# Norms of a second transformer stack: the root and the reciprocal taken per token as columns, the factor spread by a product with the identity

## What is computed

```python
def rms_norm(x, g):
    xf = x.astype(jnp.float32)
    y = xf * lax.rsqrt(jnp.mean(xf * xf, axis=-1, keepdims=True) + NORM_EPS)
    return (y * g.astype(jnp.float32)).astype(x.dtype)
def modulate(h, shift, scale):
    return h * (1 + scale) + shift
# in layer l of the second stack (ctx is only carried on in layer 0):
h  = modulate(rms_norm(x, g_mix[l]), sh1, sc1)      # 512 tokens, 1024 features
hc = modulate(rms_norm(ctx, g_mix[l]), csh1, csc1)  # 256 tokens, 1024 features
# rms_norm of c_q (384 features) and of c_kv (128 features), for x and for ctx
# modulate(rms_norm(x, g_ffn[l]), ...) before the feed-forward part
return rms_norm(x, g_final)
```

## Time and profile before

| | |
|---|---|
| median of 3 runs | 3974.38 us (3973.16 to 3976.8) |
| the profiled execution's own time | 3969.17 us |
| its span from the first to the last instruction | 3967.4 us |
| mean granted TensorE clock | 0.956 |
| PE busy | 3636.3 us, 92% |
| PEld busy | 2914.2 us, 73% |
| DVE busy | 2221.1 us, 56% |
| ACT busy | 1364.0 us, 34% |
| chain that ended last | PE 76%, DVE 12%, ACT 5% |

### The profile page before, as it was taken

One profiled execution on the slowest core, in us unless ns is written; L12 is line 12 of the kernel. 1 busy time (PEld: TensorE's weight loads), 2 busy tenths in 40 slices (PEclk: granted clock), 3 DMA queues, 4 the chain that ended last, 5 costly groups with the idle time before them and its releaser, 6 DMA issues.

```text
span 3967.4 us, 53234 instructions
## 1 busy us (share of the span) xinstructions
PE 3636.3 (92%) x19180; PEld 2914.2 (73%) x19180; DVE 2221.1 (56%) x3260; ACT 1364.0 (34%) x2104; POOL 190.7 (5%) x157
## 2 busy tenths in 40 slices
PE   8988999999998899999967998899999879879997
PEld 6755787888786578788846775688888657657876
DVE  7864456445686544744566553563535665545445
ACT  5544433222445443322212334142323233324322
POOL 2300000000230000000000000000000000000000
PEclk9988999999998999999978998999999989989998
DMA  3233332222223323222211001111111110112221
GB/s 131 85 139 120 115 113 100 96 95 95 85 86 139 139 100 113 98 95 98 94 58 53 22 21 49 43 53 64 64 64 64 54 64 22 49 64 85 93 87 74
DMA packets 44792, 325.32 MB, mean 82 GB/s; under 512 B 5088, under 2 KB 5344, under 8 KB 6112
## 3 DMA queue, kind: packets, MB, share of 16 engines
q1 hardware_dynamic: 43920, 315.88, 21.9%
q10 hardware_dynamic: 720, 7.40, 0.5%
HBM read 321.16 MB, written 2.10 MB: 81 GB/s over the span
## 4 chain that ended last, share of the span: by engine, by line
PE 76%; DVE 12%; ACT 5%; issue 3%; DVEq 3%; DMA 1%; ACTq 0%; SPq 0%
PE psum L663 10%; PE psum L665 10%; PE psum L664 10%; PE psum L1000 10%; PE psum L1002 10%; PE psum L1001 10%; PE psum L1113 3%; PE psum L1088 3%; ACT whi L1223 2%; PE psum L1099 2%; DVE wlo L1616 2%; DVE MA L1743 2%; PE psum L704 2%; PE psum L767 1%; PE psum L719 1%
## 5 line engine op out<-in xcount | busy, mean ns | idle before, releaser
L1223 ACT ACTIVATE whi<-wst 128x2048 fp32r<-128x2048 f32 x248 | 473.7, 1910 | 787.2 <-PE psum L1002 384.2
L1616 DVE TENSOR_TENSOR wlo<-wst,whi 128x2048 fp32r<-128x2048 f32 x216 | 495.0, 2291 | 197.5 <-ACT whi L1223 196.1
L663 PE MATMUL psum<-xh,whi 128*128 128x512 f32 x1328 | 525.3, 396 | 35.2 <-issue 15.1
L665 PE MATMUL psum<-xh,wlo 128*128 128x512 f32 x1328 | 519.9, 391 | 0.0
L664 PE MATMUL psum<-xl,whi 128*128 128x512 f32 x1328 | 519.7, 391 | 0.0
L1000 PE MATMUL psum<-xh,whi 128*128 128x512 f32 x944 | 380.4, 403 | 52.7 <-DVE xl L2046 40.1
L1001 PE MATMUL psum<-xl,whi 128*128 128x512 f32 x944 | 373.8, 396 | 0.0
L1002 PE MATMUL psum<-xh,wlo 128*128 128x512 f32 x944 | 373.3, 395 | 0.0
L663 PEld LDWEIGHTS psum<-xh,whi 128*128 128x128 f32 x1328 | 251.1, 189 | 99.2 <-issue 47.9
L665 PEld LDWEIGHTS psum<-xh,wlo 128*128 128x128 f32 x1328 | 251.0, 189 | 53.2
L664 PEld LDWEIGHTS psum<-xl,whi 128*128 128x128 f32 x1328 | 251.2, 189 | 52.6 <-issue 1.0
(11 more groups left out here) (300 smaller groups left out, 6570.7 us busy)
## 6 DMA issues: line engine op xcount, KB each, us to landing
wst<-weights SPq DMA_DIRECT2D x296, 1024.0 KB, 4.8
dft<-c_dft ACTq DMA_DIRECT2D x2, 2688.0 KB, 9.0
hT<-x_t SPq DMA_DIRECT2D x4, 512.0 KB, 7.5
out<-hT SPq DMA_DIRECT2D x1, 2048.0 KB, 6.3
masks<-c_masks SPq DMA_DIRECT2D x1, 1024.0 KB, 12.4
cT<-ctx_t ACTq DMA_DIRECT2D x1, 1024.0 KB, 6.4
ropes<-c_ropes ACTq DMA_DIRECT2D x1, 512.0 KB, 7.1
sm<-small ACTq DMA_DIRECT2D x1, 314.0 KB, 2.8
```

The lines of the kernel that those rows point to most:

```text
L663: pe.matmul(ps[bank][:, :], w_hi, rh[:, k + k0, :], start=n == 0, stop=False)
L665: last = pe.matmul(ps[bank][:, :], w_lo, rh[:, k + k0, :], start=False, stop=n == len(kts) - 1)
L1223: act.activation(m.whi[:, slot, :], m.wst[:, slot, :], ACT.Copy).then_inc(s.hi_ready, 1)
L1616: TT(m.wlo[:, slot, :], m.wst[:, slot, :], m.whi[:, slot, :].bitcast(F32), ALU.subtract).then_inc(s.lo_ready, 1)
```

## The change

Sums come out as columns: for each block b of 128 tokens the squares are the stationary operand and one column of ones is the moving one, which gives a 128x1 column with the tokens on the partitions. Mean, root and reciprocal work on 128x4 (or 128x2). Then PE, still inside `sums2`, waits for the reciprocal and multiplies each column, broadcast over 128 weight columns, with the identity: the factor comes out on all partitions, in bank 5, and DVE's products read it from there. The waits `rinv_ready` (PE on DVE) and `rinv_spread` (DVE on PE) are new.

```diff
+        m.var2, _ = place(nc, n_area + 8192, "var2", [P, QB])
+        m.rinv2, _ = place(nc, n_area + 8192 + 32, "rinv2", [P, QB])
...
 (PE, sums2)
                     pe.wait_ge(s.sq_ready, k0 + kt)
-                    pe.matmul(ps[4][:, 0:n], ones, m.sum2[:, c0:c0 + n], start=True, stop=True).then_inc(s.sq_used, kt)
-                    return
-                for k in range(kt):
-                    pe.wait_ge(s.sq_ready, k0 + k + 1)
-                    pe.matmul(ps[4][:, 0:n], ones, m.sq2[:, (k0 + k) % 2, 0:n], start=k == 0, stop=k == kt - 1
-                              ).then_inc(s.sq_used, 1)
+                    for b in range(n // P):
+                        last = pe.matmul(ps[4][:, b:b + 1], m.sum2[:, c0 + b * P:c0 + (b + 1) * P], ones[:, 0:1],
+                                         start=True, stop=True)
+                    last.then_inc(s.sq_used, kt)
+                else:
+                    for k in range(kt):
+                        pe.wait_ge(s.sq_ready, k0 + k + 1)
+                        for b in range(n // P):
+                            last = pe.matmul(ps[4][:, b:b + 1], m.sq2[:, (k0 + k) % 2, b * P:(b + 1) * P], ones[:, 0:1],
+                                             start=k == b == 0, stop=k == kt - 1 and b == n // P - 1)
+                        last.then_inc(s.sq_used, 1)
+                pe.wait_ge(s.rinv_ready, NORMS2[name][1] - DEPTH * NORMS1)
+                for b in range(n // P):
+                    last = pe.matmul(ps[5][:, b * P:(b + 1) * P], m.rinv2[:, b:b + 1].broadcast_to([P, P]), ident,
+                                     start=True, stop=True)
+                last.then_inc(s.rinv_spread, 1)
 (ACT, norm2)
-                act.activation(m.rstd2[:, 0:n], m.rstd2[:, 0:n], ACT.Sqrt).then_inc(s.std_ready, 1)
+                act.activation(m.var2[:, 0:n // P], m.var2[:, 0:n // P], ACT.Sqrt).then_inc(s.std_ready, 1)
 (DVE, norm2)
-                TS(m.rstd2[:, 0:n], ps[4][:, 0:n], 1.0 / width, EPS, ALU.mult, ALU.add).then_inc(s.var_ready, 1)
+                TS(m.var2[:, 0:n // P], ps[4][:, 0:n // P], 1.0 / width, EPS, ALU.mult, ALU.add).then_inc(s.var_ready, 1)
                 dve.wait_ge(s.std_ready, n0 + 1)
-                nc.vector.reciprocal(m.rstd2[:, 0:n], m.rstd2[:, 0:n])
-                dve.drain()
+                nc.vector.reciprocal(m.rinv2[:, 0:n // P], m.var2[:, 0:n // P]).then_inc(s.rinv_ready, 1)
+                dve.wait_ge(s.rinv_spread, n0 - DEPTH * NORMS1)
...
-                    STT(xn, src(k), gain(k), m.rstd2[:, 0:n], ALU.mult, ALU.mult).then_inc(s.xn_ready, 1)
+                    STT(xn, src(k), gain(k), ps[5][:, 0:n], ALU.mult, ALU.mult).then_inc(s.xn_ready, 1)
...
-                        last = STT(src(k), src(k), gain(k), m.rstd2[:, 0:n], ALU.mult, ALU.mult)
+                        last = STT(src(k), src(k), gain(k), ps[5][:, 0:n], ALU.mult, ALU.mult)
```

More of the change, by code:

```diff
@@ L482, in two_stacks @@
         m.xn2, _ = place(nc, n_area + 4096, "xn2", [P, 2, T])
-        m.rstd2, _ = place(nc, n_area + 8192, "rstd2", [P, T])
+        m.var2, _ = place(nc, n_area + 8192, "var2", [P, QB])
+        m.rinv2, _ = place(nc, n_area + 8192 + 32, "rinv2", [P, QB])
         psum = ctx.enter_context(nc.psum_tensor("psum", [P, 8 * 512], F32))
@@ L574, in two_stacks @@
         s.gl_ready = sem("gl_ready")
+        s.rinv_ready, s.rinv_spread = sem("rinv_ready"), sem("rinv_spread")
         s.final_ready = sem("final_ready")
```

## The result

The changed kernel takes 3982.64 us (median of 20 runs, 3969.41 to 3996.78), the kernel before, run beside it, 3973.84 us (20 runs). The ratio is 1.0028, 95% interval 1.0018 to 1.0038: 11 us slower, 7 to 15 with 95% (the medians are 8.8 us apart). The forecast was 3986 us, slower. Two of all runs took far longer than the rest and stand in no ratio: one of experiment 6 (5945.76 us) and one of the kernel before beside experiments 5 and 6 (10999.46 us).

What follows compares the result with a forecast made beforehand. PE, busy for 92% of the span, was taken as the bound. Terms -12.6 + 14.6 + 16.2 = +18.2 us on the profiled 3969.2; with about 6 us already in the median, +12 on 3974.4: 3986 us, range 3969 to 3993.

Steps and rivals of the forecast that it cites:

- two kinds: Fifteen norms: in seven PE or the output store waits for the products; in eight PE's next tiles are the path.
- Gains: Seven norms on the path: shorter stretch from statistics to first product, 12.6 us gained in all.
- Waits: Other eight norms: PE waits in `sums2` for reciprocal and spread while its tiles queue behind, 14.6 us lost.
- Clock: One-column sums neither raise nor hold PE's clock: 16.2 us lost, bounds 0 and 16.2 with another 2.
- (a): mix00's sums: the last four tiles go at 1.70 in place of 0.87 us, 3.3 us lost.
- (b): mix01's sums start at full clock and fall; some five of eight at half, 2.0 us lost.
- (c): Tiles behind the sums start at half clock, with a climb of 5 us in q00 and q10: 10.9 us lost.
- in the median already: Slow tiles behind the sums: 0.5 to 1 us per norm already in the old kernel's median, about 6 us.
- The clock doesn't care: Rival: new sums leave PE's clock alone, only prices remain, about -2 us, 3972.5 us; chance 0.26.
- Shorter holes keep the clock up: Rival: shorter idle before mix01's and ffn01's tiles keeps full clock, -9 us, 3965 us; chance 0.08.
- The full bill: Rival: no clock loss already in the median, attention starts low, +18 to +20, 3993 us; chance 0.06.
- A dearer factor from PSUM: Rival: 56 products on the path each a tenth longer, 4.2 us more, 3990 us; chance 0.02.

Runs made afterwards that it cites:

- experiment 6: All fifteen norms changed, sums with 128 columns of ones, and in eight the reciprocal wait and spread put six matmuls into the next tile: 3960.22 us, 0.9968 of the kernel before.
- experiment 5: Against the kernel before, only the eight norms behind whose sums PE has other tiles are changed, with sums of 128 columns: 3992.16 us, ratio 1.0040.
- experiment 2: Against the kernel before, the change only in the seven norms PE waits for (mix00, mix01, ffn00, ffn01, mix10, ffn10, final): 3963.46 us, ratio 0.9973.
- experiment 3: Against the kernel before, the change only in the other eight norms (q00, q01, kv00, kv01, mix11, q10, kv10, kv11): 3997.78 us, ratio 1.0056.
- experiment 1: The changed kernel, all fifteen norms, but sums use all 128 columns of ones as moving operand instead of one: 3972.03 us, 0.9993 of the kernel before.
- experiment 4: Against the kernel before, only the seven norms PE waits for are changed, with sums of 128 columns: 3957.32 us, ratio 0.9964.

## Why the prediction was right, point by point

**Right.** The sign, the time (3986 against 3982.64, or 3974.38 x 1.0028 = 3985.5) and the reason. The norms do fall into two kinds: experiments 2 and 3 put -11 and +22 us on them.

*Gains, forecast 12.6, measured 12.4.* Each is on its figure: 512-token norms at half clock gave 2.04 (forecast 2.05), mix01 0.83 (0.95), ffn01 1.34 (1.45). The spread of four blocks took 2.08 us at half and 1.16 at full clock (forecast 2.1 and 1.07). The three small operations and their hand-overs took 0.74 us (2040.88 to 2041.62; forecast 0.7), with the root at 205 in place of 174 ns.

*Waits, forecast 14.6, measured 10.5 to 15.* In the changed kernel's timeline PE begins the next tile 2.39 us behind the statistics of q00, kv00, q10 and kv10, 1.52 behind q01's and kv01's and 1.12 behind mix11's and kv11's: 14.9 us in all, the forecast's figure. Experiment 1 gives less: there the eight lose 10.5 us. q00 lost 1.89 and q10 1.87 us, as far as it is from the statistics to the first product at full clock (1.86); q01, kv00, mix11 and kv10 1.25 to 1.41. That figure is a low one, since in layer 1 PE was at half clock for 13.7 us against 20.5 before, which can hide up to 3.4 us (an estimate: half of the difference). Counted by the tiles' beginnings it has 12.4 us, since the spreads of q00, q01, kv01 and q10 ran at full clock there.

*Clock, forecast 16.2, measured about 9 to 13.* The lower figure takes the waits at 14.9, the upper by experiment 1. (a) mix00's sums +3.5 against 3.3, confirmed by experiment 1. (b) mix01's sums +0.4 against 2.0: the fall came as forecast, but later. The first two rows hold mix01's sums in the changed kernel, the other two its sums and the stretch behind them in experiment 1:

```profile
2062.00:2066.60 4.60, 3.09 (x25) 2.89 (x24) 3.46 (x8) 0.00 (x0) 0.00 (x0) 1.00 0.00 0
2066.60:2068.70 2.10, 1.97 (x9) 1.80 (x9) 0.57 (x3) 0.00 (x0) 0.00 (x0) 0.50 0.00 0
...
2055.80:2061.34 5.54, 4.64 (x32) 3.88 (x32) 3.33 (x9) 0.00 (x0) 0.00 (x0) 1.00 0.00 0
2061.34:2064.05 2.71, 0.71 (x4) 0.52 (x4) 1.45 (x5) 1.00 (x3) 0.00 (x0) 1.00 0.00 0
```

With one column the clock falls 2.1 us before the statistics (2068.68), and in experiment 2 too; with streamed sums, in experiment 1 and before the change, it stays up for 2.7 and 3.4 us behind them. So only the last 2.1 us ran at half, not five of eight sums, and while the clock was full the one-column sums were the quicker: two squares of 256 tokens every 1.12 us, where it was 1.22 before. The early fall costs again in mix01's spread, which ran at half. (c) the tiles behind the sums: 9.3 us (after minus experiment 1) against 10.9, but spread otherwise. q00 1.6 (forecast 2.5), q01 1.3 (2.0), q10 2.0 (2.5): the climb "of 5 us ahead of it" took 2.1 us of q00's tile (0.50 until 2114.41). This climb is the step that was sized too large. And mix11 lost 1.4 and kv11 1.5, where the forecast had none.

*Why 18.2 became 11.* The second stack of the profiled pair lost 9.4 us where the sum said 18.2: 5.7 too much in the eight (waits and clock together), 1.4 in the sums of mix00 and mix01, and 1.9 that came back in untouched code. Norm by norm the eight, forecast and measured (from each one's statistics to the next mark, after minus before), are: q00 4.9 and 3.5, q01 3.5 and 2.7, kv00 3.4 and 2.3, kv01 2.8 and 2.8, mix11 1.1 and 2.8, q10 4.9 and 3.9, kv10 3.4 and 1.2, kv11 1.5 and 0.7. The forecast then took 6 us off for rises "in the median already", with q00 called lucky in the profile of before. No run shows such a term, and q00 was not lucky: experiments 2 and 4, which leave it as it was, show the same, 14.1 and 14.2 us from its statistics to q01's without any half clock. What the 6 us did was to make up for oversized terms. That the number on record was nearer than its working is luck.

*The rivals.* "The clock doesn't care" (3972.5) is refuted by experiment 1, where only the columns differ and mix00's sums get 3.5 us back; its time turned up in experiment 1, where the new sums treat the clock as the old ones did. "Shorter holes keep the clock up": the changed kernel fails its test, since mix01's spread ran at half. Experiments 1 and 4 meet the first half of its condition, mix01's spread at full clock and 1.40 us, and just miss the second: in experiment 1 the clock fell at 2064.1 us and the first tile began at 2064.43. Its 3 us in the tiles behind did not come, 38.84 against 39.27 us from mix01's first product to q00's statistics. A small form of it is there behind ffn10, as told under the table of the result. The full bill did not come. *A dearer factor from PSUM*: the product with the factor in PSUM took 747 ns (32 of 128x512), the one without 751. The Trainium skill's page "VectorE: DVE Perf Modes" (section on the TRN2 errata) has a fixed 120 cycles in place of 58 for an operation that reads PSUM, an estimate of 65 ns more at its 0.96 GHz. This case's trace does not agree.

*The marks that were named ahead.* First product 2.85 us behind the statistics in mix00 and 1.91 in mix01 (forecast 1.3 to 1.9). q00's tiles 2.4 us behind. Clock 0.50 in all of mix00's sums. DVE's idle time before the copy 4.75 us, a little under the 5 that was named. Half clock at the start of q00's tiles for 2.1 us, not 5.

## What to carry to other kernels

Before speeding up a small serial chain, ask for each place where it stands who waits for its end: here seven of fifteen were worth 11 to 14 us, and the other eight cost 16 to 22 (each known to 5 to 8 us either way), because the cheaper chain used the engine that was the bound and put a wait at the head of its queue. Where the bound engine has to take part in such a chain, let it issue a piece of the next work first (six matmuls ahead of each of eight waits took 8 us of loss away in the profile, 10 by the ratios). And on TensorE the shape with the least arithmetic is not the fastest: a sum with one moving column left the clock at half where 128 columns of the same sum let it rise.

## What was not expected of the hardware

- 128 moving columns in place of one, 512 in all per sum, made the kernel 11 us faster by the medians (3982.64 to 3972.03) and 14 by the ratios (1.0028 to 0.9993), though PE streams more. At half clock both shapes go at the same pace: the squares come every 1.70 us with either, and in mix00's sums the weight loads are busy for all of PE's time (10.96 of 11.00 us after, 5.44 of 5.44 in experiment 1's half-clock part). At full clock the wider product is not free: two squares of 256 tokens took 1.22 us in place of 1.12 in mix01.
- The same first stack took 2016.3 to 2025.5 us in eight profiled executions, with 105 to 133 us of it at half clock. Two profiles can differ by 9 us in code that nobody touched; a change of this size must be read from marks within the changed part.
- A read of the factor from PSUM by a product of 128x512 cost nothing: 747 against 751 ns, and 480 against 484 for 128x256.
